# Group norm of three head pairs woven into the last state chain; the samples normalised apart; three sample updates on GpSimd

## The reference, cut to what matters

```python
def step(S, inp):                       # 8 heads of 64; the prompt in chunks of 64 rows
    sa = einsum('bhvk,bhk->bhv', S, -kk_t)
    S = S * w_t[:, :, None, :] + sa[..., None] * (kk_t * a_t)[:, :, None, :] + v_t[..., None] * k_t[:, :, None, :]
    return S, einsum('bhvk,bhk->bhv', S, r_t)
...
mu = mean(o, -1); var = mean(square(o - mu), -1)          # per head: the group norm
o = ((o - mu) * rsqrt(var + RWKV_GN_EPS)) * rwkv_ln_w + rwkv_ln_b
bonus = sum(rf * kf * r_k, -1) * vf
out = (o + bonus) * g                                      # g = sigmoid(gd) @ rwkv_g_up
mix = concatenate([out, y_swa], -1) @ w_out                # then norm, residual, ConvFFN
```

## Time and profile before

| quantity | us |
|---|---|
| median of 3 runs | 1609.4 |
| lowest and highest | 1608.08, 1611.38 |
| profiled execution, its own time | 1612.83 |
| profiled execution, span of the trace | 1611.0 |
| TensorE busy | 1432.5 (89%) |
| VectorE busy | 831.5 (52%) |
| ScalarE busy | 549.8 (34%) |
| GpSimd busy | 125.4 (8%) |

### The profile page before, as it was taken

The page is one execution under the profiler, slowest core; times in us unless marked ns, Lnnn a source line. Parts: engine busy times, 40 slices in busy tenths (PEclk is TensorE's granted clock), DMA queues, the critical chain, the costliest instruction groups (busy, mean ns, idle before and its releaser), DMA issues.

```text
span 1611.0 us, 28834 instructions
## 1 busy us (share of the span) xinstructions
PE 1432.5 (89%) x12458; PEld 1325.7 (82%) x12458; DVE 831.5 (52%) x1080; ACT 549.8 (34%) x748; POOL 125.4 (8%) x204
## 2 busy tenths in 40 slices
PE   4799999677489876779888999999999999999995
PEld 1699999444377775479768999999999999999994
DVE  2742333565477777452565545545455454454557
ACT  3311211454466541521554141222313223232244
POOL 0000000000022120112411000000000000000006
PEclk7899999788699997789989999999999999999998
DMA  9332111443000010112313111111111111111114
GB/s 345 121 91 67 53 40 40 147 165 112 1 3 4 4 37 30 53 40 119 108 50 111 52 40 39 52 52 45 46 39 52 41 37 65 39 52 39 40 53 147
DMA packets 38249, 107.61 MB, mean 67 GB/s; under 512 B 5560, under 2 KB 17608, under 8 KB 37248
## 3 DMA queue, kind: packets, MB, share of 16 engines
q1 hardware_dynamic: 38160, 106.30, 19.0%
HBM read 93.29 MB, written 11.40 MB: 65 GB/s over the span
## 4 chain that ended last, share of the span: by engine, by line
PE 74%; DVE 15%; ACT 4%; issue 3%; DMA 2%; POOL 0%; DVEq 0%; SPq 0%; ACTq 0%; POOLq 0%
PE ps L542 47%; PE ps L981 11%; PE ps L696 3%; DMA raw<-ada 2%; PE ps L523 2%; PE ps L908 2%; DVE Z L2098 1%; PE ps L674 1%; PE ps L589 1%; PE ps L604 1%; PE ps L618 1%; DVE acc L2132 1%; PE ps L1008 1%; PE ps L817 1%; PE ps L531 1%
## 5 line engine op out<-in xcount | busy, mean ns | idle before, releaser
L542 PE MATMUL ps<-XS,spl 128*128 128x344 f32 x4824 | 766.9, 321 | 21.4 <-DVE spl L1651 10.1
L542 PEld LDWEIGHTS ps<-XS,spl 128*128 128x128 f32 x4824 | 764.2, 190 | 22.8 <-issue 11.3
L981 PE MATMUL ps<-act,spl 128*128 128x344 f32 x1440 | 230.7, 320 | 0.8
L981 PEld LDWEIGHTS ps<-act,spl 128*128 128x128 f32 x1440 | 226.8, 188 | 3.3 <-DVE acc L2132 3.3
L2098 DVE SCALAR_TENSOR_TENSOR Z<-U,par,Z 128x1023 f32<-128x1023 f32 x86 | 110.3, 1283 | 151.1 <-ACT Z L1423 145.5
L1377 ACT ACTIVATE spl<-raw 128x1024 fp32r<-128x1024 f32 x66 | 68.7, 1055 | 282.2 <-PE ps L981 198.4
L2132 DVE TENSOR_TENSOR acc<-acc,ps 128x1032 f32<-128x1032 f32 x80 | 98.3, 1229 | 112.1 <-PE ps L981 112.0
L1651 DVE TENSOR_TENSOR spl<-raw,spl 128x1024 fp32r<-128x1024 f32 x28 | 34.2, 1224 | 163.4 <-ACT spl L1081 163.4
L2029 DVE TENSOR_TENSOR spl<-raw,spl 128x1024 fp32r<-128x1024 f32 x66 | 80.5, 1233 | 58.3 <-ACT spl L1377 57.1
L1081 ACT ACTIVATE spl<-raw 128x1024 fp32r<-128x1024 f32 x28 | 29.6, 1059 | 215.8 <-PE ps L542 215.8
L1420 ACT ACTIVATE U<-ps 128x1032 f32<-128x1032 f32 x43 | 44.3, 1029 | 149.9 <-PE ps L542 145.6
(11 more groups left out here) (316 smaller groups left out, 1652.5 us busy)
## 6 DMA issues: line engine op xcount, KB each, us to landing
raw<-ada SPq DMA_DIRECT2D x48, 512.0 KB, 5.3
raw<-up SPq DMA_DIRECT2D x44, 512.0 KB, 3.4
raw<-down SPq DMA_DIRECT2D x22, 512.0 KB, 3.8
raw<-w_in SPq DMA_DIRECT2D x20, 512.0 KB, 3.6
xT<-xT SPq DMA_DIRECT2D x4, 1032.0 KB, 11.8
X<-xT SPq DMA_DIRECT2D x1, 4128.0 KB, 13.0
x_dram<-X SPq DMA_DIRECT2D x3, 1376.0 KB, 5.6
o_y<-acc SPq DMA_DIRECT2D x24, 172.0 KB, 2.0
```

What stands on the lines that cost most here:

```text
L542: mm = nc.tensor.matmul(ps[:, 3 * bank_set + t, 0:SL], w[:, a, k * P:(k + 1) * P], x[:, k, b, t * SL:(t + 1) * SL], start=(k == order[0] a ...
L981: mm = nc.tensor.matmul(ps[:, 3 * (y % 2) + t, 0:SL], w[:, a, k * P:(k + 1) * P], act2[:, f, b, t * SL:(t + 1) * SL], start=(f == 0 and n ...
```

## The change

- The order behind pair 3 is a table written by hand, `LAST`, in place of `order(NJ)`'s filter. Between the 16 chain steps stand the means, variances and gates of pairs 0 to 2 in single slices (`mean0` to `mean8` and so on; TensorE), `centre`, `scale`, `shift`, `gated` (VectorE), `square`, `log`, `std` (ScalarE), the splits of the four attention tiles (`ahi`, `alo`) and of `w_out`'s first two tiles (`whi`, `wlo`). Pair 3's own norm stands behind the table.
- `alo` is now VectorE's work (it was GpSimd's, 4 operations). Sample updates 5, 6 and 7 are GpSimd's (they were VectorE's); VectorE's reduction (`sum_samples`) waits for them and stands after chain step 6.
- `normalised` is two operations (`scale` and `shift`, both with two full inputs in SBUF) and no longer three.
- The samples' columns (T to N) of the norm are a line of their own on 32 columns (`turn_out`, `take_out`, `mean_samples` to `lo_samples`); the last pair's gate and low rest cover 1024 columns.
- `w_out`'s tiles 0 and 1 are loaded earlier, into `out_raw`, after pair 3's J3 products. The product's first two tiles are issued in pieces: rows 4 to 7, then 0, 1, 2, and row 3 of tile 0 after rows 4 to 7 of tile 1.
- Semaphores of the sample attention become one counter; work rows `XG` lie elsewhere.

```diff
+        POOL_STEPS = range(5, 8)
+        LAST = [(a.rstrip("0123456789"), int(a[len(a.rstrip("0123456789")):])) for a in (
+            "chain0 mean0 mean1 whi0 chain1 mean2 mean3 ahi4 chain2 mean4 mean5 centre0 square0 wlo0 chain3 mean6 mean7 "
...
             if j == NJ:
-                return [x for x in pieces if x[0] in of_chain]
+                return LAST
...
-                        if x[0] not in ("decay", "rate", "scan", "bonus", "norm", "floor", "root", "expr"):
+                        if x[0] in ("kf", "rkk", "kk", "exps", "alpha"):
                             out.append(("update", n))
...
             state(2)
+            sp.wait_ge(*nth("j3_out", 2 * NJ))
+            for n in range(2):
+                dma(out_raw[:, n], io["w_out"][n], s("first_out"))
             sp.wait_ge(s("sample_o"), 1)
...
+            def last_gate():
+                j = NJ - 1
+                pe.wait_ge(s("o_done"), 2 * NJ)
+                pe.wait_ge(s("sample_norm"), SAMPLE_AT["log"])
+                for half in range(2):
+                    mm = nc.tensor.matmul(ps[:, 6 + half, :], g_up[:, j * P:(j + 1) * P],
+                                          PT[:, 13, PO + 512 * half:PO + 512 * half + 512], start=True, stop=True)
+                mm.then_inc(s("gn_gate"), 1)
...
+            def out_rows(n, rows):
+                bank_set = n % 2
+                for k in rows:
+                    if n == 0:
+                        if k == 0:
+                            pe.wait_ge(s("sample_norm"), SAMPLE_AT["low"])
+                        pe.wait_ge(*mixed(k))
+                    for term, (a, b) in enumerate(((0, 0), (0, 1), (1, 0))):
...
+            for t in range(3):
+                gn_mean(NJ - 1, t)
+            pe.wait_ge(w_lo, PC + 1)
+            pe.wait_ge(s("gated"), 3)
+            out_rows(0, MIX_ORDER[0:2])
+            for t in range(3):
+                gn_var(NJ - 1, t)
+            out_rows(0, MIX_ORDER[2:6])
+            last_gate()
+            out_rows(0, MIX_ORDER[6:7])
+            pe.wait_ge(w_lo, PC + 2)
+            pe.wait_ge(s("gn_log"), NJ)
+            out_rows(1, MIX_ORDER[0:4])
+            out_rows(0, MIX_ORDER[7:8]).then_inc(s("out_ready"), 1)
+            out_rows(1, MIX_ORDER[4:8]).then_inc(s("out_ready"), 1)
...
-            for j in range(NJ):
-                pool.wait_ge(s("mix_hi_a"), j + 1)
-                nc.gpsimd.tensor_tensor(XS[:, 4 + j, 1], PT[:, 14 + j, PO:PW], XS[:, 4 + j, 0].bitcast(F32), ALU.subtract
-                                        ).then_inc(s("mix_lo_a"), 1)
+            for n in POOL_STEPS:
+                if n == POOL_STEPS[0]:
+                    pool.wait_ge(s("sample_step"), 1)
+                    step = nc.gpsimd.tensor_tensor(sTmp, over_k(V32), over_v(2), ALU.mult)
+                elif n == POOL_STEPS[1]:
+                    pool.wait_ge(s("sample_step"), 2)
+                    step = nc.gpsimd.tensor_tensor(sWKV, sWKV, sTmp, ALU.add)
+                else:
+                    pool.wait_ge(s("sample_step"), 3)
+                    step = nc.gpsimd.tensor_tensor(sTmp, sWKV, over_v(4), ALU.mult)
+                step.then_inc(s("sample_step"), 1)
...
+            def sum_samples():
+                dve.wait_ge(s("sample_step"), 1 + len(POOL_STEPS))
+                nc.vector.tensor_reduce(Osm[:], sTmp, AX.X, ALU.add).then_inc(s("sample_o"), 1)
...
+            def scale(j):
+                Y = PT[:, j, PO:PW]
+                dve.wait_ge(s("gn_std"), j + 1)
+                link(nc.vector.scalar_tensor_tensor(Y, Y, param("rwkv_ln_w", j), XG[j], ALU.mult, ALU.mult))
+
+            def shift(j):
+                Y = PT[:, j, PO:PW]
+                link(nc.vector.scalar_tensor_tensor(Y, Y, param("rwkv_ln_b", j), PT[:, 4 + j, PO:PW], ALU.add, ALU.add))
...
+            def mix_low_a(k):
+                dve.wait_ge(s("mix_hi_a"), k - 3)
+                nc.vector.tensor_tensor(XS[:, k, 1], PT[:, 10 + k, PO:PW], XS[:, k, 0].bitcast(F32), ALU.subtract
+                                        ).then_inc(s("mix_lo_a"), 1)
```

More of the change, by code:

```diff
@@ L253, in build_program @@
         HEADS = (slice(0, HD), slice(HD, P))
-        SAMPLE_STEPS = 9
+        POOL_STEPS = range(5, 8)
+        ATT_AT = {step: n + 1 for n, step in enumerate(("keys_turned", "keys_out", "scored", "scores_out", "scores_turned", "probs", "probs_turned", "probs_out", "valued", "mixed"))}
+        SAMPLE_AT = {step: n + 1 for n, step in enumerate(("turned", "gate", "out", "mean", "centred", "square", "var", "log", "std", "y",
+                                                           "hi", "low"))}
         PREP = ("decay", "rate", "norm", "floor", "root", "kf", "rkk", "kk", "bonus", "scan", "expr", "exps", "alpha", "kappa", "beta",
@@ L467, in _ @@
             sp.wait_ge(s("mix_lo_r"), NJ)
+            sp.wait_ge(s("sample_norm"), SAMPLE_AT["low"])
             dma(X2[:], io["xT"], s("x2_in"))
@@ new lines, in hi_samples, with whi_out @@
+            def hi_samples():
+                act.wait_ge(s("sample_norm"), SAMPLE_AT["y"])
+                act.wait_ge(s("gated"), 3)
+                nc.scalar.activation(XS[:, 0:NJ, 0, T:N], SCEN, ACT.Copy).then_inc(s("sample_norm"), 1)
+            def whi_out(n):
+                if n < 2:
+                    act.wait_ge(s("first_out"), 32)
+                    if n == 1:
+                        act.wait_ge(w_lo, PC + 1)
+                    nc.scalar.activation(spl[:, n, 0], out_raw[:, n], ACT.Copy).then_inc(w_hi, 1)
+                else:
+                    early = 1 if n % 4 < 2 else 0
+                    act.wait_ge(raw_in[n % 4], ((ADA_A + ADA_B + PC + n) // 4 + 1 - early) * 16)
+                    whi(n % 2, n % 4)
@@ L1273, in _ @@
                         sample_attention(x)
+                    elif j == NJ:
+                        if piece == "square":
+                            gn_square(x)
+                        elif piece == "log":
+                            gn_log(x)
+                        elif piece == "std":
+                            gn_std(x)
+                        elif piece == "ahi":
+                            mix_hi_a(x)
+                        elif piece == "rhi":
+                            mix_hi_r(x)
+                        elif piece == "whi":
+                            whi_out(x)
+                        elif piece == "take_out":
+                            take_out()
+                        elif piece == "square_samples":
+                            square_samples()
+                        elif piece == "log_samples":
+                            log_samples()
+                        elif piece == "std_samples":
+                            std_samples()
+                        elif piece == "hi_samples":
+                            hi_samples()
@@ L1935, in _ @@
                         chain(j - 1, x)
-                        if j == NJ and x == 1:
-                            sample(SAMPLE_STEPS - 1)
                     elif piece == "outer":
                         outer(j - 1, x)
+                    elif j == NJ:
+                        if piece == "sum_samples":
+                            sum_samples()
+                        elif piece == "centre":
+                            centre(x)
+                        elif piece == "scale":
+                            scale(x)
+                        elif piece == "shift":
+                            shift(x)
+                        elif piece == "gated":
+                            gated(x)
+                        elif piece == "rlo":
+                            mix_low_r(x)
+                        elif piece == "alo":
+                            mix_low_a(x)
+                        elif piece == "wlo":
+                            low_out(x)
+                        elif piece == "centre_samples":
+                            centre_samples()
+                        elif piece == "scale_samples":
+                            scale_samples()
+                        elif piece == "lo_samples":
+                            lo_samples()
@@ L1970, in _ @@
-            centre(0)
-            centre(1)
-            centre(2)
-            normalised(0)
-            centre(3)
-            gated(0, 1)
-            normalised(1)
-            gated(1, 1)
-            normalised(2)
-            gated(2, 0)
-            mix_low(0)
-            normalised(3)
-            low_out(0)
-            gated(3, 1)
-            for j in range(1, NJ):
-                mix_low(j)
-            low_out(1)
+            centre(NJ - 1)
+            scale(NJ - 1)
+            shift(NJ - 1)
```

337 lines of the change are left out of this document (187 added, 150 removed), and 5 rows, old and new, of the table LAST.

## The result

The changed kernel takes 1583.12 us (median, 1580.9 to 1587.96) against 1609.89 (1608.08 to 1611.38) of the kernel before, run beside it: ratio 0.9838, 95% interval 0.9813 to 0.9863, 26.8 us faster. The forecast was 1583.4. The profiled execution took 1583.28 us, with a span of 1581.5.

A forecast was written before the change was run, and what follows sets the result against it. TensorE (74% busy) bounds the kernel, so time is won only where it waits, chiefly 620 to 696.73 us. The walk's -27.7 with 1.7 charged for the clock gave -26: 1583.4 us, range 1578 to 1595.

The forecast's parts named there:

- Updates off VectorE (6.0): Last chain's start: without three sample updates on VectorE, copy 0 stands at 623.4 instead of 629.4, worth 6.0 us.
- The woven chain (copy 15 at 656.9, +10.6): Last state chain woven with norm pieces: 1.7 us per step with two norm matmuls, copy 15 10.6 us later.
- GpSimd (3.9 each, and a block of 3.5 on `wlo` 0): Three updates on GpSimd from 620.0 to 631.7, 3.9 us each; `wlo` 0 on VectorE waits 3.5 for the third.
- the nearest row: Profile row used for GpSimd's updates: a broadcast multiply of 1024 elements in 1.93 us, so 3.9 for 2048.
- First product at 664.5, then a wait of 3.2: First output product starts when the third `gated` ends, 664.5; TensorE then waits 3.2 us for pair 3's square.
- the walk: Step-by-step timing from the updates to two finished products, assuming 2.4 GHz throughout: 27.7 us earlier.
- Two products done at 694.2: End of the first two output products: 29.6 us after 664.5, at 694.2 against 721.9 before.
- The sum: Whole kernel: -27.7 by the walk, 1.7 charged for the clock, result -26, so 1583.4 us.
- the charge of 1.7 for the clock: Allowance for TensorE's low clock in the woven stretch; 10 us at low clock would cost 4, 1.7 was charged.
- Hidden things: Row 3 of tile 0 hidden with 3.6 us to spare; samples' round trip 6.7 to 8.4 us, taken as costing nothing.
- The clock did fall: Clock rival: TensorE at 1.2 GHz until about 670, two products done at 707, -14.5, 1594.9 us; chance 0.20.
- The slower rival: GpSimd's updates hold the reduction and the chain behind it; at 18 us per update 1617 us; chance 0.04.

The follow-up runs named there:

- both unwoven runs: Changed kernel with the weave undone, all chain steps first; samples' reduction behind step 6 (1597.14 us, 0.9922) or step 13 (1592.95 us, 0.9875).
- both of the kernel before: Kernel before with updates 5 to 7 on GpSimd; samples' reduction behind chain step 1 (1612.72 us, 1.0006) or step 10 (1602.39 us, 0.9943).
- late `alo`: Changed kernel with `alo` 4 moved behind step 10 and `alo` 5 behind `turn_out`: 1579.89 us, ratio 0.9816.
- the run with dummies: Changed kernel plus five TensorE matmuls of 344 columns, results unread, behind step 13 and the outer products: 1579.75 us, ratio 0.9800.
- in one run and not in the other: Five dummy matmuls added to the changed kernel (1579.75 us, 0.9800), or to it with `alo` late and pair 3's square early (1574.87 us, 0.9760).

## Why the prediction was right

**Updates off VectorE (6.0).** Copy 0 was forecast at 623.4 and stood at 623.66, 6.3 us nearer to update 4 than before. Taken back alone, the part costs 5.2: the 6.3, 1.5 more in step 1 at a low clock, and 2.7 less for the block of `alo` 4.

**The woven chain (copy 15 at 656.9, +10.6).** It stood at 656.30; counted from update 4 it came 9.6 us later than before and not 10.6. The 1.7 us for a step with two norm matmuls were 1.73. What the forecast did not say is how much the weave was worth by itself: 11.0 by the traces, 6 by the ratios.

**GpSimd (3.9 each, and a block of 3.5 on `wlo` 0).** Two sizes and the place were off. The updates took 3.62, 4.52 and 5.42: only the first, whose two inputs are both broadcast, was like the nearest row. Where no such VectorE operation ran ahead of it the third took 4.49 to 4.53 (both unwoven runs and both of the kernel before). `wlo` 0 came 0.30 us ahead of the third update and ran its 1.31; GpSimd was the one that lost 0.9, and lost it with late `alo` too (5.42). The block then fell on `alo` 4, which started at 631.30 and took 2.96 more than its 1.22. So the price was 3.0 and not 3.5, and moving `alo` 4 and 5 won copy 15 3.3 us. The Trainium skill (SBUF — State Buffer, "SBUF: two separate sides") says that whichever of the two starts first holds the shared port pair for its whole instruction; the trace agrees in both directions, with 5.42 for 4.50 on GpSimd and 4.18 for 1.22 on VectorE. The Trainium skill (GPSIMD Engine Reference, "3.1 Elementwise — side-by-side cycle accounting") has 4497 ns for such an operation of 2048 elements, which the 4.50 and 4.52 here agree with; I had gone by the nearest row instead.

**First product at 664.5, then a wait of 3.2.** The first product began at 666.30: 0.6 of the 1.8 us come from a later update 4, and 1.2 are what is left of two errors. At full clock it would have come 3.05 us sooner (the run with dummies), so the low clock cost 3.05 and the walk itself was 1.9 too late: 1.65 of it in the chain (35.28 us from update 4 to copy 15's end with dummies, 36.93 forecast), 0.2 a slip in its sum (656.9 + 7.4 is 664.3). Nor did the first product wait for the third `gated` alone, as forecast: that ended at 665.55, but TensorE was still at pair 3's mean, 3.78 us at the low clock (1.97 with dummies), and began the product 0.75 us later. The wait for the square was 0.35 in place of 3.2, because the 18 matmuls ahead of it took 4.57 instead of 2.82 and started later, while pair 3's `centre` ended about where the walk had it (670.07 against 669.4, 0.6 of it from ahead of update 4). So the terms were off by 2 to 3 us each and cancelled: the low clock largely filled a wait that stands there at full clock, as the 2.50 us of the run with dummies show.

**Two products done at 694.2.** 694.78 stood in the trace, 0.6 of it from ahead of update 4. **The sum** was met although its parts were off: the charge of 1.7 for the clock was too high (the dummies give only 0.7 back, net), and the wait of 3.2 was all but absent. The forecast of 26 was met by the median (26.8); by distance it was 27.75, against the 27.7 of the walk without that charge, and that agreement is partly luck, since the errors above cancelled.

**Hidden things.** Row 3 of tile 0 was hidden: pair 3's low part was done at 684.29 (forecast 683.6), and putting the row ahead of tile 1 uncovers a wait of 2.41. The round trip of the samples took 7.9 us at most (reduction's end 640.22, `turn_out` at 648.12), with TensorE busy until 648.19 with the gate ahead of it: nothing, as taken.

**The rivals.** The clock did fall, but at 650 and not through the chain, and it cost under 1 us instead of 11.5: TensorE ran 4.9 us of 5 in the stretch before, and the fall came with matmuls of 8 columns from 648.12 on and short waits for VectorE behind steps 12 to 14 (0.40, 0.67 and 0.69 us). Dummies behind step 13 and later kept it at 1.00 in one run and not in the other, so what sets the fall off is open. The slower rival (GpSimd holds the reduction) was ruled out by slack, not by mechanism: behind step 1 of the kernel before, GpSimd's updates make the reduction wait 8.74 us and eat the whole gain. In the changed kernel the reduction started 3.6 us after GpSimd had ended.

## What to carry to other kernels

When two chains of small operations use different engines at half load, weave them and judge by when the last consumer starts, not by when the first chain ends: here the chain ended 17 us later than unwoven and the first two products were done 11 us sooner, by the traces. Work given to a slow engine is worth what the place of its consumer in the other queue makes it (0 or 8.6 us here), and operations that contend with it for SBUF belong behind its end. After each gain look which wait comes next: a full clock and an unblocked VectorE both ran into the same wait for pair 3's square, and moving its two entries in the table was worth 3 us by the traces.

## What was not expected of the hardware

GpSimd can be the loser at the port as well: its third update took 5.42 us with a VectorE operation of two SBUF inputs started 0.30 us ahead of it, 4.50 without. A VectorE operation that reads PSUM kept 1.22 us beside it. An operation of 2048 elements whose two inputs are both broadcast took GpSimd 3.62 us, one with a full input and nothing in its way 4.49 to 4.53; on VectorE both took 2.29. The granted clock stayed at 1.00 with TensorE 3.00 and 3.94 of 5 us busy (635 to 640 and 630 to 635 in the changed kernel), and was 0.61 with 4.34 busy from 655 to 660, so the busy share of a stretch alone did not tell which clock it had.
